# Router logits taken from the rows before the first layer norm, and the first expert's down-projection loads held until the first gather has landed

## The chip, the cores and the metric

One core of a Trainium2 chip runs the whole kernel. The metric is device time in microseconds (us) of one execution; lower is better. The engines are TensorE (PE, with its weight loads listed apart as PEld), VectorE (DVE), ScalarE (ACT), GpSimd (POOL, which here issues transfers and builds gather indices) and SyncE (SP, which here only issues transfers).

## The reference, cut to what matters

Two sequences of 512 rows of 1024 floats go through one encoder layer. The part that the change touches is this:

```python
x = layer_norm(DEEPNORM_ALPHA * x + jnp.dot(mixed, w_out), ln1_g, ln1_b)
x = layer_norm(DEEPNORM_ALPHA * x + grouped_moe(x, ...), ln2_g, ln2_b)

def layer_norm(x, g, b):        # over the 1024 columns of a row
    return (x - mu) * rsqrt(var + 1e-5) * g + b

def grouped_moe(x, w_router, router_bias, w_gate, w_up, w_down):
    scores = sigmoid(dot(x, w_router))          # 16 experts
    ...                                         # best of 4 groups, best 2 experts in it
    for e in range(16):
        h = silu(dot(x, w_gate[e])) * dot(x, w_up[e])
        y = y + combine[:, e:e+1] * dot(h, w_down[e])
```

With y a row ahead of the first norm, w_router the matrix W, and g and b the gain and bias, the router's logits are `rstd * (y @ (g*W) - mean * (g @ W)) + b @ W`: they can be had from the row ahead of the norm, once its mean and its reciprocal root are known.

## The kernel before, in words

All matmuls run on operands that were split into a high and a low float32r part, so each product is three matmuls (high by high, high by low, low by high: lines 1402 to 1404). ACT makes the high part with a cast, DVE the low part with a subtraction.

A sequence is 4 tiles (t = 0..3) of 128 rows. `schedule()` writes one list of events by hand; each engine's program walks this list and issues what the event means on that engine, in that order, so the list is each engine's program order. The two sequences follow one another (s = 0, 1). Within one: 18 weight chunks of projections (`C` events in quarters, with `P` events preparing the next chunk: ACT's cast at L922, DVE's subtraction at L1168), 32 steps p of attention, two heads' blocks each (`S` scores at L1437, maximum on DVE at L1178 or L1192, exponential on ACT at L945 or L950, `T` transposes of the probabilities at L1547 with their copy by ACT at L540, `PV` at L1572), and the output projection (`W` events: 2 halves of 512 columns x 4 weight chunks `pi` x 4 tiles; six matmuls each). Behind the last chunk of a half, `Y` events on DVE add the projection to the residual row in `x_nat` (L1272) and take its statistics (L1275).

The layer norm is a `VAR` event (DVE: mean and variance of 4 tiles, L1301 and L1302, and a chain of small instructions for the reciprocal root, L1127 to L1132) and four `LN` events (DVE, L1309 and L1310, 1024 columns each; POOL then stores the tile to `x1_dram`, L830). In ACT's program the `LN` events of sequence 1 carry the casts of the first expert's first 8 weight units (L931).

The router of a tile is three units: two `r` units (PE transposes four 128-column blocks of the normed row into a PSUM bank, L1466; ACT copies the bank to `x1T`, L1027) and one `R` unit (8 matmuls by `wr`, L1582, which the trace lists as 16; ACT copies 16 logits to `sc`, L1037). These units share two PSUM banks T0 and T1 in rotation with the `T` units, and a unit waits until ACT has emptied its bank. For sequence 0 the router's units stand in steps 2 to 10 of sequence 1; for sequence 1 they stand behind its `LN` events. Then ACT takes the sigmoid of all logits (L1040), and DVE's `routing` (L590 to L675) builds the index lists; its first instruction waits for the sigmoid and for all stores of `x1_dram`.

Behind it comes the expert stage. POOL copies the first indices (L849) and gathers 128 rows of 1024 floats from `x1_dram` into `x_nat` (L846). PE transposes them (L1608), ACT and DVE split them (L1046, L1325), and PE runs the 48 gate and up matmuls (L1402 to L1404) and the 24 down matmuls (L1644) of a tile. An expert's weights are 12 units of 512 KB: 4 of `w_gate`, 4 of `w_up` (units 0 to 7), 4 of `w_down` (units 8 to 11). There is one raw buffer for each unit: SP loads unit w of expert e+1 (L713, L717) when DVE has split unit w of expert e (L1319). SP's issues are in order. For the first expert, units 0 to 7 are loaded during the attention of sequence 1, and unit 8 waits for the index lists:

```python
                if w == KD:
                    sp.wait_ge(routed, 1)
                load_unit(0, w)
```

At the end the experts' outputs are gathered back, combined and normed, and the rows are stored.

Of the kernel before, what the change touches and what calls it, by code (L numbers as in the profile page):

```python
# [89 lines left out]
def schedule():  # L90
# [42 lines left out]
    for s in range(NSEQ):  # L133
# [10 lines left out]
        for p in range(NP + 1):  # L144
# [68 lines left out]
        for pi in range(4):  # L213
# [13 lines left out]
    return ev, tu[0]  # L227


EVENTS, N_TU = schedule()  # L230
# [8 lines left out]
R_UNITS = {(s, t): [e[4] for e in EVENTS if e[0] == "r" and e[1:3] == (s, t)] for s in range(NSEQ) for t in range(NT)}  # L239


def build_kernel(nc, x, mem, w_in, w_mem_kv, sink, rpb, grp_g, w_out, ln1_g, ln1_b, w_router, router_bias,
                 w_gate, w_up, w_down, ln2_g, ln2_b, out):
    with ExitStack() as ctx:
# [77 lines left out]
        mvv = sb("mvv", [P, 12, 2])  # L322
# [4 lines left out]
        sc = sb("sc", [P, TT, NE])  # L327
        idxc = sb("idxc", [P, 1], I32)
# [73 lines left out]
        x1_stored = sem("x1_stored")  # L402
        sig_done = sem("sig_done")
# [164 lines left out]
        def routing(dve, link):  # L568
# [19 lines left out]
            dve.wait_ge(sig_done, 1)  # L588
# [92 lines left out]
        def _(sp):  # L681
# [65 lines left out]
        def _(pool):  # L747
# [50 lines left out]
            for ev in EVENTS:  # L798
# [32 lines left out]
                elif what == "R" and s == 0 and ev[2] == NT - 1:  # L831

                    pool.wait_ge(x1_stored, 16 * NT)
                    for t in range(NT):
                        for u in R_UNITS[(0, t)]:
                            pool.wait_ge(t_ready[u % 2], u // 2 + 1)
                        pool.dma_start(x_nat[:, t, :], x[1][t * P:(t + 1) * P, :]).then_inc(x_again[t], 16)
# [70 lines left out]
        def _(act):  # L908
# [48 lines left out]
            for ev in EVENTS:  # L957
# [64 lines left out]
                elif what == "r":  # L1022
                    t, b, u = ev[2], ev[3], ev[4]
                    act.wait_ge(t_ready[u % 2], u // 2 + 1)
                    if t == 0 and b == 0:
                        act.wait_ge(vb_stored, 16 * 8 * (s + 1))
                    nc.scalar.activation(x1T[t % 2][:, 4 * b:4 * b + 4, :], Tb[u % 2][:, :].rearrange("p (k c) -> p k c", k=4),  # L1027
                                         ACT.Copy).then_inc(t_drained[u % 2], 1)
                elif what == "LN" and s == NSEQ - 1:
# [3 lines left out]
                    hi_units(0, 0, (2 * t, 2 * t + 1))  # L1033
                elif what == "R":
                    t, u = ev[2], ev[3]
                    act.wait_ge(t_ready[u % 2], u // 2 + 1)
                    nc.scalar.copy(sc[:, s * NT + t, :], Tb[u % 2][:, 0:NE]).then_inc(t_drained[u % 2], 1)  # L1037
# [78 lines left out]
        def _(dve):  # L1116
# [87 lines left out]
            for ev in EVENTS:  # L1204
# [94 lines left out]
                elif what == "VAR":  # L1299
                    for t in range(NT):  # L1300
                        link(nc.vector.bn_aggr(mvv[:, t, :], stats[:, t, :, :].rearrange("p a b -> p (a b)")))  # L1301
                    link(nc.vector.tensor_scalar(nv[:, 0:NT], mvv[:, 0:NT, 1], EPS, None, ALU.add))  # L1302
                    rsqrt(rstd[:, s * NT:(s + 1) * NT], NT)
                elif what == "LN":
# [4 lines left out]
                    link(nc.vector.scalar_tensor_tensor(row, row, mvv[:, t, 0:1], ln[:, 0, :], ALU.subtract, ALU.mult))  # L1309
# [87 lines left out]
        def _(pe):  # L1397
# [43 lines left out]
            for ev in EVENTS:  # L1441
                what, s = ev[0], ev[1]
                if what in ("x", "m", "oA", "oM", "oB", "r"):
# [18 lines left out]
                    else:  # L1462
                        pe.wait_ge(x1_ready, s * NT + t + 1)
                        src = [x_nat[:, t, (4 * ev[3] + k) * P:(4 * ev[3] + k + 1) * P] for k in range(4)]
# [110 lines left out]
                elif what == "R":  # L1575
# [4 lines left out]
                    pe.wait_ge(t_drained[u % 2], u // 2)  # L1580
                    for k in range(KD):
# [95 lines left out]
```

## Time and profile before

| | us |
|---|---|
| median of 3 runs | 1092.63 |
| the 3 runs | 1094.33, 1087.12, 1092.63 |
| time of the profiled execution | 1090.34 |
| its span in the profile | 1088.8 |
| busy in the span: PE / DVE / ACT / POOL | 908.7 / 636.7 / 522.3 / 138.3 |

The profile is of one execution. Times in it count from the start of the span; the time of the execution is 1.5 us longer than the span. Matmuls are pipelined: a row gives how long one was in the array, and the step from one start to the next is shorter.

### The profile page before, as it was taken

The page shows a single profiled execution, that of the slowest core. Times are in us where ns is not written, and L with a number is a line of the kernel's source. Part 1 is how long each engine was busy: PE and PEld are TensorE (multiplying, and loading weights), DVE is VectorE, ACT ScalarE, POOL GpSimd, SP SyncE. Part 2 cuts the span into 40 slices and gives each one's busy share as a digit, 9 for nine tenths or more (in the row PEclk, how much of TensorE's full clock was granted, in tenths as well). Part 3 has the DMA queues.
Part 4 walks back from the last instruction along what each step waited for, and adds up shares of the span by engine and source line. Part 5 has one row for each costly group of instructions (what it writes and reads, how often), then busy time and mean ns, then how long its engine had stood idle before and what let it go on. Part 6 is the DMA issues. An engine that isn't in the chain of part 4 may idle for free.

```text
span 1088.8 us, 15827 instructions
## 1 busy us (share of the span) xinstructions
PE 908.7 (83%) x4892; PEld 754.1 (69%) x4893; DVE 636.7 (58%) x1184; ACT 522.3 (48%) x974; POOL 138.3 (13%) x202
## 2 busy tenths in 40 slices
PE   6799999899799999896619999999999999998000
PEld 6677888778688887775617788787878787877000
DVE  5335545466364445566368888875457664461696
ACT  4334554533355555533108787855447464452310
POOL 3200010010000010000010000000000000003775
PEclk9999999899999999898558999999999999999555
DMA  7822132053334123025259999995676966656811
GB/s 233 149 42 71 47 85 90 20 193 99 89 85 155 40 79 97 20 68 191 90 185 337 393 396 401 391 395 175 210 259 219 352 204 228 210 193 223 316 79 77
DMA packets 113404, 195.58 MB, mean 180 GB/s; under 512 B 23137, under 2 KB 52032, under 8 KB 113360
## 3 DMA queue, kind: packets, MB, share of 16 engines
q1 hardware_dynamic: 97296, 139.48, 37.4%
q0 software_dynamic: 12752, 43.47, 12.2%
q10 hardware_dynamic: 3312, 12.06, 2.7%
q8 instruction: 25, 0.41, 0.2%
q14 instruction: 19, 0.16, 0.0%
HBM read 167.71 MB, written 27.65 MB: 179 GB/s over the span
## 4 chain that ended last, share of the span: by engine, by line
PE 55%; DVE 11%; ACT 2%; DMA 2%; issue 2%; POOL 0%; ACTq 0%; DVEq 0%; POOLq 0%
PE O L1644 12%; PE C L1402 10%; PE C L1403 10%; PE C L1404 10%; PE O L1572 3%; PE T L1608 2%; PE T L1582 2%; PE S L1437 2%; DVE mixing L1375 1%; PE T L1547 1%; PE T L1466 1%; DVE mixing L1374 1%; DVE split_aux L1340 1%; DMA x_nat<-x_dram,idxc 1%; ACT split_aux L1059 1%
## 5 line engine op out<-in xcount | busy, mean ns | idle before, releaser
L1319 DVE TENSOR_TENSOR split_main<-mixing,split_main 128x1024 fp32r<-128x1024 f32 x192 | 220.8, 1218 | 50.7 <-ACT split_main L931 50.1
L931 ACT CAST split_main<-mixing 128x1024 fp32r<-128x1024 f32 x192 | 189.4, 1048 | 34.0 <-PE C L1404 18.3
L1402 PE MATMUL C<-split_main,split_aux 128*128 128x512 f32 x368 | 144.3, 392 | 2.6 <-DVE split_aux L1325 2.6
L1644 PE MATMUL O<-split_main,split_aux 128*128 128x512 f32 x552 | 132.3, 395 | 16.2 <-DVE split_aux L1340 16.2
L1404 PE MATMUL C<-split_main,split_aux 128*128 128x512 f32 x368 | 144.1, 392 | 0.0
L1403 PE MATMUL C<-split_main,split_aux 128*128 128x512 f32 x368 | 144.1, 392 | 0.0
L1402 PE MATMUL C<-split_main 128*128 128x512 f32 (+1 forms) x320 | 129.6, 405 | 9.7 <-DVE split_main L1219 6.3
L1644 PEld LDWEIGHTS O<-split_main,split_aux 128*128 128x128 f32 x552 | 101.8, 188 | 42.4 <-DVE split_aux L1340 21.6
L1403 PE MATMUL C<-split_main 128*128 128x512 f32 (+1 forms) x320 | 121.0, 378 | 0.0
L1404 PE MATMUL C<-split_main 128*128 128x512 f32 (+1 forms) x320 | 120.6, 377 | 0.0
L1402 PEld LDWEIGHTS C<-split_main 128*128 128x128 f32 x320 | 62.7, 196 | 28.8 <-issue 10.9
L1402 PEld LDWEIGHTS C<-split_main,split_aux 128*128 128x128 f32 x368 | 69.7, 190 | 17.5 <-issue 3.0
L1404 PEld LDWEIGHTS C<-split_main,split_aux 128*128 128x128 f32 x368 | 69.7, 189 | 14.6
L1403 PEld LDWEIGHTS C<-split_main,split_aux 128*128 128x128 f32 x368 | 69.7, 189 | 14.5
L540 ACT COPY probsT<-T 128x256 f32<-128x256 f32 (+1 forms) x128 | 46.0, 401 | 60.9 <-PE T L1547 59.2
L950 ACT ACTIVATE probs<-probs,negm 128x256 f32<-128x256 f32 (+1 forms) x96 | 51.5, 538 | 49.0 <-DVE negm L1192 49.0
L1404 PEld LDWEIGHTS C<-split_main 128*128 128x128 f32 x320 | 62.2, 194 | 11.3
L1403 PEld LDWEIGHTS C<-split_main 128*128 128x128 f32 x320 | 62.7, 196 | 8.2
L1192 DVE CUSTOM_DVE_ANT_0 probs<-S,mixing,nsink 128x256 f32<-128x256 f32 (+1 forms) x64 | 32.7, 548 | 56.3 <-PE S L1437 56.1
L1168 DVE TENSOR_TENSOR split_main<-mixing,split_main 128x1024 fp32r<-128x1024 f32 x36 | 44.0, 1225 | 36.4 <-ACT split_main L922 36.3
L1335 DVE TENSOR_TENSOR x_nat<-x_nat,C 128x256 f32<-128x256 f32 x46 | 17.3, 417 | 70.7 <-PE C L1404 70.7
L1059 ACT CAST split_aux<-S 128x256 fp32r<-128x256 f32 x46 | 14.9, 375 | 85.1 <-PE S L1633 85.1
(240 smaller groups left out, 1409.0 us busy)
## 6 DMA issues: line engine op xcount, KB each, us to landing
mixing<-in_w_gate SPq DMA_DIRECT2D x64, 512.0 KB, 7.7
mixing<-in_w_up SPq DMA_DIRECT2D x64, 512.0 KB, 5.6
mixing<-in_w_down SPq DMA_DIRECT2D x64, 512.0 KB, 7.3
y_dram<-x_nat ACTq DMA_DIRECT2D x23, 512.0 KB, 6.7
mixing<-in_w_in SPq DMA_DIRECT2D x20, 512.0 KB, 3.8
mixing<-in_w_out SPq DMA_DIRECT2D x16, 512.0 KB, 3.8
y_dram<-x_nat POOLq DMA_DIRECT2D x18, 256.0 KB, 4.3
mixing<-in_w_mem_kv SPq DMA_DIRECT2D x8, 512.0 KB, 3.8
```

What stands on the lines that cost most here:

```text
L540: copy(probsT[:, a % 2, 0:w], Tb[u % 2][:, 0:w]).then_inc(t_drained[u % 2], 1)
L931: nc.scalar.copy(wu[0][:, w, :], raw[:, w, :]).then_inc(unit_hi, 1)
L950: nc.scalar.activation(pr[:, 0:w], pr[:, 0:w], ACT.Exp, scale=-1.0, bias=negm[:, gi % 2, j:j + 1], accum_out=sums[:, gi % 2, j:j + 1]).the ...
L1059: nc.scalar.copy(dst, src).then_inc(hT_hi, 1)
L1168: ins = nc.vector.tensor_tensor(wch[1][:, slot, :, :], wraw[:, slot], wch[0][:, slot, :, :].bitcast(F32), ALU.subtract)
L1192: nc.vector.tensor_tensor_reduce(out=probs[:, a % 2, 0:w], in0=Sb[a % 2][:, 0:w], in1=bias, scale=-1.0, scalar=start, op0=ALU.add, op1=ALU ...
L1319: nc.vector.tensor_tensor(wu[1][:, w, :], raw[:, w, :], wu[0][:, w, :].bitcast(F32), ALU.subtract).then_inc(unit_lo, 1)
L1402: ins = nc.tensor.matmul(out_ap, st[0], mvg[0], start=first, stop=False)
L1403: ins = nc.tensor.matmul(out_ap, st[0], mvg[1], start=False, stop=False)
L1404: ins = nc.tensor.matmul(out_ap, st[1], mvg[0], start=False, stop=last)
L1572: ins = nc.tensor.matmul(Ob[gi % 2][:, j * HD:(j + 1) * HD], probsT[:, a % 2, k * P:(k + 1) * P], v, start=(k == 0), stop=(k == len(vs) - 1))
L1644: ins = nc.tensor.matmul(Ob[half][:, :], st[a_], wu[b_][:, KD + f, half * 512:(half + 1) * 512], start=(f == 0 and a_ + b_ == 0), stop=(f ...
```

## The change

The router's units work on `x_nat` ahead of the norm. In sequence 1's tail they stand between the last `W` events, a tile's `r` units one tile behind its projection and its `R` unit two behind, and `VAR` and `LN` come after all of them. The router's weights are `wr` times the gain (`wrg`); a pseudo sequence `GB`, whose two tiles are the gain and the bias, already broadcast over the partitions, gives the gain's columns and the two constants `g @ W` and `b @ W` (`scon`). It runs in steps 0 to 2 of sequence 1. Sequence 0's own units move to steps 3 to 10, a tile's two `r` units in the same step, and `VAR` from step 1 to 2, its `LN` from 1, 3, 5, 7 to 4, 6, 8, 10. An `SC` event corrects the logits on DVE in four instructions of 128x64: for sequence 0 at step 12, for sequence 1 between `LN` of tile 0 and `LN` of tile 1; in ACT's program the sigmoid of all logits stands there too. A sigmoid of one column (`warm`) is put ahead of ACT's first router copy of sequence 1. SP's wait ahead of unit 8 of the first expert is for the first gather instead of the index lists. The order of POOL's issues changes in one place only (the reload of `x_nat` goes from behind the last `R` of sequence 0 to behind its last `LN`).

```diff
@@ schedule(), in the steps p of a sequence
             if s > 0:
-                if p == 1:
+                if p < 2:
+                    router(GB, p, 0)
+                    router(GB, p, 1)
+                if p in (1, 2):
+                    router(GB, p - 1, 2)
+                if p == 2:
+                    ev.append(("GW", s))
                     ev.append(("VAR", s - 1))
                 for t in range(NT):
-                    if p == 2 * t + 1:
+                    if p == 2 * t + 3:
+                        router(s - 1, t, 0)
+                        router(s - 1, t, 1)
+                    if p == 2 * t + 4:
+                        router(s - 1, t, 2)
                         ev.append(("LN", s - 1, t))
-                    if 0 <= p - (2 * t + 2) < 3:
-                        router(s - 1, t, p - (2 * t + 2))
+                if p == 12:
+                    ev.append(("SC", s - 1))
@@ schedule(), the end of a sequence and of the list
-        for pi in range(4):
+        for pi in range(3 if s + 1 == NSEQ else 4):
             wo(s, 1, pi, WO_ORDER[1], True)
...
-    ev.append(("VAR", NSEQ - 1))
+    s = NSEQ - 1
+    for t in range(NT + 2):
+        if t < NT:
+            wo(s, 1, 3, (t,), t == NT - 1)
+        if t > 0 and t - 1 < NT:
+            router(s, t - 1, 0)
+            router(s, t - 1, 1)
+        if t > 1:
+            router(s, t - 2, 2)
+    ev.append(("VAR", s))
     for t in range(NT):
-        ev.append(("LN", NSEQ - 1, t))
-    for t in range(NT + 1):
-        if t < NT:
-            for b in range(2):
-                router(NSEQ - 1, t, b)
-        if t > 0:
-            router(NSEQ - 1, t - 1, 2)
+        ev.append(("LN", s, t))
+        if t == 0:
+            ev.append(("SC", s))
@@ routing (DVE)
-            dve.wait_ge(sig_done, 1)
+            dve.wait_ge(sig_done, 2)
@@ loads of the first expert (SP)
                 if w == KD:
-                    sp.wait_ge(routed, 1)
+                    sp.wait_ge(xg_loaded, 16)
@@ ACT
+                    if s == NSEQ - 1 and t == 0 and b == 0:
+                        act.wait_ge(vb_stored, 16 * 8 * NSEQ)
+                        nc.scalar.activation(warm[:, :], seed[:, 0:1], ACT.Sigmoid).then_inc(sig_done, 1)
                     nc.scalar.activation(x1T[t % 2][:, 4 * b:4 * b + 4, :], ..., ACT.Copy).then_inc(t_drained[u % 2], 1)
...
+                elif what == "SC" and s == NSEQ - 1:
+                    act.wait_ge(logits_ready, NSEQ)
+                    nc.scalar.activation(sc[:, :, :], sc[:, :, :], ACT.Sigmoid).then_inc(sig_done, 1)
...
-            for b in range(2):
-                act.wait_ge(t_drained[b], (N_TU - 1 - b) // 2 + 1)
-            nc.scalar.activation(sc[:, :, :], sc[:, :, :], ACT.Sigmoid).then_inc(sig_done, 1)
@@ DVE
+                elif what == "GW":
+                    t_waits(dve, R_UNITS[(GB, 0)][1])
+                    nc.vector.tensor_tensor(wrg[:, :, :], wr[:, :, :], x1T[0][:, :, 0:1].to_broadcast([P, KD, NE]), ALU.mult)\
+                        .then_inc(gains_ready, 1)
+                elif what == "SC":
+                    t_waits(dve, T_OF_R[(s, NT - 1)])
+                    raw_, mean = sc[:, s * NT:(s + 1) * NT, :], mvv[:, 12:12 + NT, 0]
...
+                    link(nc.vector.tensor_tensor(sct, over_t[0], mean, ALU.mult))
+                    link(nc.vector.tensor_tensor(sct, raw_, sct, ALU.subtract))
+                    link(nc.vector.tensor_tensor(sct, sct, rs, ALU.mult))
+                    nc.vector.tensor_tensor(raw_, sct, over_t[1], ALU.add).then_inc(logits_ready, 1)
                 elif what == "LN":
                     t = ev[2]
+                    for u in R_UNITS[(s, t)]:
+                        dve.wait_ge(t_ready[u % 2], u // 2 + 1)
@@ PE
-                        pe.wait_ge(x1_ready, s * NT + t + 1)
-                        src = [x_nat[:, t, ...] for k in range(4)]
+                        if s == GB:
+                            pe.wait_ge(ln_loaded, 32)
+                        else:
+                            pe.wait_ge(wo_drained, wo_done(s, 1, t))
+                        rows = (ln if s == GB else x_nat)[:, t, :]
+                        src = [rows[:, ...] for k in range(4)]
...
-                        ins = nc.tensor.matmul(Tb[u % 2][:, 0:NE], x1T[t % 2][:, k, :], wr[:, k, :],
+                        ins = nc.tensor.matmul(Tb[u % 2][:, 0:NE], x1T[t % 2][:, k, :], (wr if s == GB else wrg)[:, k, :],
```

## Rows read from the trace of the kernel before

**Rows 1.** The page, the span in 40 slices of 27.2 us: granted clock and DMA share.
```profile
PEclk9999999899999999898558999999999999999555
DMA  7822132053334123025259999995676966656811
```

**Rows 2.** Timeline, tail of sequence 1 (start, us; in brackets the idle time before).
```profile
503.18 0.39 PE L1402 MATMUL S<-split_main 128*128 128x512 f32 x1
...
505.34 0.69 DVE L1272 SCALAR_TENSOR_TENSOR x_nat<-x_nat,S 128x512 f32<-128x512 f32 x1
...
506.79 0.94 DVE L1301 BATCH_NORM_AGGREGATE mvv<-stats 128x2 f32<-128x12 f32 x4
...
510.14 1.28 DVE L1309 SCALAR_TENSOR_TENSOR x_nat<-x_nat,mvv,ln 128x1024 f32<-128x1024 f32 x1
...
517.27 3.57 PE L1582 MATMUL T<-wr,vstg 128*128 128x16 f32 x16
...
519.01 1.28 DVE L1310 SCALAR_TENSOR_TENSOR x_nat<-x_nat,rstd,ln 128x1024 f32<-128x1024 f32 x1
...
535.10 1.28 ACT L1040 ACT_TABLE_LOAD   x1
```

**Rows 3.** Timeline, from the routing's start to the first expert's matmuls.
```profile
537.04 0.48 DVE L590 MEMSET x_nat<- 128x512 f32 x1 [16.20 <-ACT sc L1040]
...
556.47 0.06 DVE L675 MEMSET seed<- 128x1 f32 x1
556.56 2.01 SPq L717 DMA_DIRECT2D mixing<-in_w_down  x4
...
558.00 1.72 POOL L846 DMA_INDIRECT x_nat<-x_dram,idxc  x1 [0.29 <-POOL idxc L849]
...
568.03 1.94 PE L1608 MATMUL T<-ident,x_nat 128*128 128x128 f32 x8 [12.07 <-DMA x_nat<-x_dram,idxc]
...
572.53 0.79 PE L1402 MATMUL C<-split_main,split_aux 128*128 128x512 f32 x1 [2.57 <-DVE split_aux L1325]
```

**Rows 4.** Chain that ended last, two of its pieces (start, us, what).
```profile
558.00 9.89 DMA x_nat<-x_dram,idxc
...
588.13 5.78 PE O L1644 x24
```

**Rows 5.** Windows: busy us (and count) of PE, PEld, DVE, ACT, POOL, then clock, DMA, GB/s.
```profile
296.00:298.00 2.00, 0.27 (x2) 0.15 (x2) 1.48 (x3) 0.77 (x3) 0.00 (x0) 1.00 0.01 2
...
508.00:510.00 2.00, 0.00 (x0) 0.00 (x0) 1.66 (x11) 2.00 (x3) 0.00 (x0) 0.87 0.00 0
510.00:512.00 2.00, 0.00 (x0) 0.00 (x0) 1.93 (x3) 2.00 (x3) 0.00 (x0) 0.50 0.00 0
...
574.00:576.00 2.00, 2.00 (x6) 1.62 (x5) 2.00 (x3) 1.98 (x2) 0.00 (x0) 0.50 0.95 355
```

**Rows 6.** Timeline, sequence 0's router units in the steps of sequence 1.
```profile
308.65 0.60 ACT L1027 ACTIVATE vstg<-T 128x512 f32<-128x512 f32 x1
...
311.77 0.60 PE L1466 MATMUL T<-ident,x_nat 128*128 128x128 f32 x4
...
317.00 1.85 PE L1582 MATMUL T<-wr,vstg 128*128 128x16 f32 x16
```

**Rows 7.** Waits of PE from 293 to 350 us (in total, times, longest).
```profile
PE T L1547 <- ACT probs L945: 1.7, 1, 1.7
PE T L1547 <- ACT vstg L1027: 0.9, 1, 0.9
```

**Rows 8.** Windows, 300 to 350 us (columns as in rows 5).
```profile
300.00:350.00 50.00, 49.14 (x340) 41.95 (x340) 27.86 (x56) 26.80 (x74) 4.24 (x8) 1.00 0.33 107
```

**Rows 9.** DMA issues from 500 to 545 us (count, KB each, median us to landing).
```profile
x_dram<-x_nat POOLq DMA_DIRECT2D x4, 512.0 KB, 3.0
```

**Rows 10.** DMA issues from 555 to 600 us.
```profile
x_nat<-x_dram,idxc POOLq DMA_INDIRECT x3, 6.6
```

**Rows 11.** DMA from 600 to 640 us, all queues.
```profile
DMA packets 6442, 16.01 MB, mean 400 GB/s; under 512 B 488, under 2 KB 488, under 8 KB 6441
```

**Rows 12.** Timeline of ACT, the second expert's weight casts.
```profile
589.07 5.93 ACT L931 CAST split_main<-mixing 128x1024 fp32r<-128x1024 f32 x6 [0.20 <-issue]
```

More of the change, by code:

```diff
@@ L238 @@
 LAST_M = [max(e[4] for e in EVENTS if e[0] == "m" and e[1] == s) for s in range(NSEQ)]
-R_UNITS = {(s, t): [e[4] for e in EVENTS if e[0] == "r" and e[1:3] == (s, t)] for s in range(NSEQ) for t in range(NT)}
+R_UNITS = {(s, t): [e[4] for e in EVENTS if e[0] == "r" and e[1:3] == (s, t)] for s in range(NSEQ + 1) for t in range(NT)}
 def build_kernel(nc, x, mem, w_in, w_mem_kv, sink, rpb, grp_g, w_out, ln1_g, ln1_b, w_router, router_bias,
@@ L327, in build_kernel @@
         sc = sb("sc", [P, TT, NE])
+        wrg = sb("wrg", [P, KD, NE])
+        scon = sb("scon", [P, 2, NE])
+        sct = sb("sct", [P, NT, NE])
+        warm = sb("warm", [P, 1])
         idxc = sb("idxc", [P, 1], I32)
@@ L830, in _ @@
                     pool.dma_start(x1_dram[(s * NT + t) * P:(s * NT + t + 1) * P, :], x_nat[:, t, :]).then_inc(x1_stored, 16)
[L831 to L837, printed above, removed]
+                    if s == 0 and t == NT - 1:
+                        pool.wait_ge(x1_stored, 16 * NT)
+                        for t in range(NT):
+                            pool.dma_start(x_nat[:, t, :], x[1][t * P:(t + 1) * P, :]).then_inc(x_again[t], 16)
             pool.dma_start(ln[:, 0, :], ln2_g.partition_broadcast(P)).then_inc(ln2_loaded, 16)
@@ L1300, in _ @@
                     for t in range(NT):
-                        link(nc.vector.bn_aggr(mvv[:, t, :], stats[:, t, :, :].rearrange("p a b -> p (a b)")))
-                    link(nc.vector.tensor_scalar(nv[:, 0:NT], mvv[:, 0:NT, 1], EPS, None, ALU.add))
+                        link(nc.vector.bn_aggr(mvv[:, 12 + t, :], stats[:, t, :, :].rearrange("p a b -> p (a b)")))
+                    link(nc.vector.tensor_scalar(nv[:, 0:NT], mvv[:, 12:12 + NT, 1], EPS, None, ALU.add))
                     rsqrt(rstd[:, s * NT:(s + 1) * NT], NT)
+                elif what == "GW":
[5 more added lines that the diff above has]
+                    raw_, mean = sc[:, s * NT:(s + 1) * NT, :], mvv[:, 12:12 + NT, 0]
+                    rs = rstd[:, s * NT:(s + 1) * NT]
+                    over_t = [scon[:, i, :].unsqueeze(1).to_broadcast([P, NT, NE]) for i in range(2)]
+                    link(nc.vector.tensor_tensor(sct[:, :, :], over_t[0], mean.unsqueeze(2).to_broadcast([P, NT, NE]), ALU.mult))
+                    link(nc.vector.tensor_tensor(sct[:, :, :], raw_, sct[:, :, :], ALU.subtract))
+                    link(nc.vector.tensor_tensor(sct[:, :, :], sct[:, :, :], rs.unsqueeze(2).to_broadcast([P, NT, NE]), ALU.mult))
+                    nc.vector.tensor_tensor(raw_, sct[:, :, :], over_t[1], ALU.add).then_inc(logits_ready, 1)
                 elif what == "LN":
                     t = ev[2]
+                    for u in R_UNITS[(s, t)]:
+                        dve.wait_ge(t_ready[u % 2], u // 2 + 1)
                     if s == 0 and t == 0:
@@ L1462, in _ @@
                     else:
-                        pe.wait_ge(x1_ready, s * NT + t + 1)
-                        src = [x_nat[:, t, (4 * ev[3] + k) * P:(4 * ev[3] + k + 1) * P] for k in range(4)]
+                        if s == GB:
[3 more added lines that the diff above has]
+                        rows = (ln if s == GB else x_nat)[:, t, :]
+                        src = [rows[:, (4 * ev[3] + k) * P:(4 * ev[3] + k + 1) * P] for k in range(4)]
                     for k, part in enumerate(src):
```

16 lines of the change are left out of this document (11 added, 5 removed).

## The prediction

> **What bounds the kernel now.** I read the page's slices first. PE's clock stands at its high level nearly everywhere, and the one deep hole ahead of the end is the 20th and 21st, 517 to 571 us [rows 1]. So I read the timeline there. The last six matmuls of the output projection start at 503.18 and PE's dense work is over 1.4 us later, at 504.6: 24 such matmuls take 5.78 us, 0.24 each [rows 4]. It begins again with the first expert at 572.53 [rows 3]. These 68 us are one serial path, and what the change does to the time is decided there. Its first part, from the last `Y` on DVE (505.34) to the routing's first instruction (537.04), takes 31.7 us: `Y` 1.45, `VAR` from 506.79 to 510.14, four `LN` from 510.14 to 520.29, then the router's units at PE's half clock, with 3.57 us for 16 entries of `R`, and a table load of 1.28 ahead of the sigmoid [rows 2, 3]. DVE waits 16.2 us for that sigmoid [rows 3]. The second part is the routing on DVE, 537.04 to 556.5, which stays as it is. The third is the first gather, 9.89 us from issue to landing, with the transposes and splits behind it [rows 3, 4]. PE waits 12.07 us for it. The gather is issued 1.4 us behind four loads of `w_down`, on other queues [rows 3].
>
> The other place that the change touches is the start of sequence 1's attention. There PE is the bound: busy 49.14 of 50 us from 300 to 350, with only 2.6 us of waits from 293 to 350 [rows 7, 8]. Work added to PE there costs its full length; DVE (27.86 of 50) and ACT (26.80) have room.
>
> **Part 1, the tail of sequence 1.** At the high clock, `r` is four transposes of 0.60 together and `R` 1.85, both less some 0.15 that runs on under the next instruction (0.39 in the array against a step of 0.24): 0.45 and 1.70. ACT's copy of a bank is 0.60 [rows 2, 4, 6]. Ahead of the last tile's matmuls PE now does `r` twice for tiles 0 and 1 and `R` of tile 0: 4 x 0.45 + 1.70 = 3.5. Two banks serve them all, so the second pair waits for ACT, whose first copy is behind the new table load (1.28 and a short sigmoid); most of that load passes under tile 2's matmuls, and I put 1.1 for the waits. So the last matmul ends at 504.6 + 4.6 = 509.2 and the last `Y` starts at 509.35, 4.0 later than before. From there: `Y` 1.45, `VAR` 3.35, `LN` of tile 0 2.55, to 516.7. PE meanwhile does `r` twice for tiles 2 and 3, `R` three times and some bank waits, 7.7 us, and its last logits are out at 517.3; DVE waits 0.7 for them. Four small `SC` instructions: 1.0 (estimate; the trace of before has none of 128x64). Three `LN`: 7.6. Then POOL's store of the last tile, 0.35 until it is issued and 3.0 to its landing [rows 9], which was hidden under the router before and is now what ends last. That is 509.35 + 1.45 + 3.35 + 2.55 + 0.7 + 1.0 + 7.6 + 3.35 = 529.4 against 537.04: **7.6 us less**. The sigmoid is not late: the two casts ahead of it on ACT and itself take some 2.3 us, while DVE is in its three `LN`. POOL's queue has nothing ahead of the store. Bounds: 5 (waits on the banks doubled, `SC` twice as long) to 9.5 (no bank waits, store landing in 2).
>
> The clock decides whether these units cost 0.45 and 1.70 or twice that. In the tail of before PE stood still from 504.9, and its clock fell only between 508 and 510 (mean 0.87), to the low level from 510 [rows 5]. A stop of 1.7 us at 296 left it at 1.00 [rows 5]. In the changed order no stop is that long until the last `R`, so I count with the high level.
>
> **Part 2, the first gather alone.** With SP's wait, the four `w_down` loads and the second expert's loads behind them on SP start after the landing. The store of the same 512 KB lands in 3.0 with nothing beside it [rows 9]; three gathers of this kernel under load have a median of 6.6 [rows 10]. Alone it lies between 3.0 and 6.6; I take 3.5, near the lone store, with 0.5 for the longer issue (1.72 [rows 3]): **6.4 us less** (3.3 to 6.9).
>
> A rule of the Trainium skill speaks against so much: in DMA: Bandwidth & Descriptors (section Queues, rings and completion order) each DMA engine goes round the queues that have work, packet by packet. By it the gather would get about half of the engines beside SP's stream, and holding the loads would save only the other half; that is the first rival below.
>
> What the hold costs: the loads start at the landing G instead of some 11 us ahead of it, and PE starts 4.6 us behind G (572.53 - 567.89 [rows 3, 4]). A unit of 0.524 MB takes 1.31 us at the 400 GB/s of rows 11. The last unit of the second expert is the seventeenth transfer (16 units, one gather): G + 17 x 1.31 + 1.7 for the landing (3.0 - 1.31 [rows 9]) = G + 24. ACT cast the last of these units some 21.5 us behind PE's start [rows 3, 12], G + 26. So it is 2 us in time; at the 355 GB/s seen from 574 to 576 [rows 5] it is 17 x 1.48 + 1.7 = G + 26.9, 0.9 late. I put 0.5 lost (0 to 4).
>
> **Part 3, gain and bias through the router's units.** Four `r` and two `R` more on PE: 4 x 0.45 + 2 x 1.70 = 5.2. Two `r` fall into PE's wait of 1.7 at step 0 [rows 7], 0.9 back; but the first probabilities then wait for ACT's two copies, about 1.0, and the first `R` for its bank, 0.5. The stop of 0.9 behind an `r` copy [rows 7] goes, since no `r` stands in step 2 any more. Together **4.8 us more**. Bounds: 2.6 (all of rows 7 filled) to 8 (0.6 more in each of the four steps with two `r`, where a copy is behind a weight cast on ACT). `GW` (0.3), `SC` (1.0) and the later `VAR` and `LN` lie in DVE's free half [rows 8]. PE stays the bound from there to the sequence's end, so the shift passes through.
>
> **The sum.** 7.6 + 6.4 - 4.8 - 0.5 = 8.7 us less than the profiled execution's 1090.34 (span 1088.8 and 1.5 around it): 1081.6. This execution is 2.3 under the median of the runs, 1092.63; from the median it is 1083.9. I say 1082.5.
>
> **Rivals.** (a) The gather was slow by itself, not by its neighbours: for it speaks its POOL time of 1.72 and that gathers between loads have 6.6, not 9.9 [rows 3, 10]; against it the lone store's 3.0. At half of 400 GB/s for 0.524 MB the neighbours cost 1.3: 1090.34 - 7.6 - 1.3 + 4.8 + 0.5 = 1086.7.
> (b) The clock falls in the tail, as it did before: the units between and behind the projection then take twice as long, 3.5 + 7.7 more, and the last projection tiles 2.8. The last logits come near 528.5 instead of 517.3, and DVE's `SC`, three `LN` and the store end at 540.5, 3.5 later than before: 1090.34 + 3.5 - 6.4 + 4.8 + 0.5 = 1092.7, no gain. Against it: rows 5, as above.
> (c) The other side: the weights become the bound of the expert stage. An expert with one tile moves 12 units, a gather and a store, 14 x 0.524 = 7.34 MB, while PE needs 72 x 0.24 = 17.3 and about 1.3 for transposes and waits, 18.6. So below 395 GB/s the transfers are slower than PE. Before, they ran ahead by what was loaded during the gather; that lead is what the change spends. At 355 to 365 GB/s an expert takes 20.4, 1.8 more, and the six full slices of DMA, the 22nd to the 27th [rows 1], hold about 9 of them: 16 us, 1090.34 - 8.7 + 16 = 1097.6. Against it: 400 GB/s held over 40 us [rows 11].
> (d) The shift of part 3 is at its upper end and the tail's waits on two banks at theirs: 5 + 6.4 - 8 - 0.5, 1087.4.
>
> **Chances.** Forecast 0.63, (a) 0.12, (b) 0.07, (c) 0.06, (d) 0.12. The forecast's own range is 1076 to 1088; with (a), (b) and (d) the range is 1075 to 1092. A difference of 1%, 10.9 us, is about what a measurement of this kernel can tell from no change. The forecast lies just inside it, and about half of its spread beyond: faster 0.34; slower 0.05, of (c); same 0.61.
>
> **What would show it.** Right: matmuls of the router between those of the last projection tiles, at clock 1.00 until 516; the routing's first instruction near 529, released by a store; the gather at 3 to 4 us; `w_down` issued behind its landing; no wait of PE for DVE's weight splits in the first three experts; the first scores behind step 3 some 5 us later than before. Wrong: the sigmoid still releasing the routing, a gather above 6, PE waiting on L1319 in the expert stage, or a clock of 0.50 before 516.

## The result and the profile after

| | before | after |
|---|---|---|
| median | 1090.70 us (17 runs) | 1096.09 us (17 runs) |
| lowest to highest | 1087.12 to 1094.74 | 1092.87 to 1100.62 |
| profiled execution, its span | 1090.34, 1088.8 | 1095.57, 1093.8 |

The changed kernel takes 1.0047 of the time before, with a 95% interval of 1.0033 to 1.0061: 5.4 us slower by the medians, where 8 to 10 less had been forecast, and outside the range. The two profiled executions differ by as much, 5.0 of span. Cut at the same events, the two traces say where:

| stretch | before | after | difference | forecast |
|---|---|---|---|---|
| start to the first scores of sequence 1 | 293.9 | 297.8 | +3.9 | 0 |
| first scores of step 0 to those of step 12 | 67.0 | 73.7 | +6.7 | +4.8 |
| step 12 to the first `Y` of the tail | 139.8 | 140.5 | +0.7 | 0 |
| first `Y` to the routing's first instruction | 36.4 | 32.0 | -4.4 | -7.6 |
| the routing | 19.4 | 19.4 | 0 | 0 |
| routing's end to the transposes of the gathered rows | 11.6 | 6.5 | -5.1 | -6.4 |
| from there to the first expert's first matmul | 4.5 | 4.5 | 0 | 0 |
| that matmul to PE's last of the experts | 431.7 | 435.5 | +3.8 | +0.5 |
| the end | 84.6 | 84.0 | -0.7 | 0 |

The first line is in code that the change doesn't touch. There the clock fell once more in this execution (from 94 to 100 us it was at 0.50); other executions of the same code have that fall (experiments 4 and 6) or not (1 and 3). It is a reminder that a term of 2 us can't be read from one execution's end time, only at its own place.

**The tail.** Timeline of the kernel after, PE and DVE mixed (answers to rows 2; columns as there):

```profile
516.77 1.93 PE L1627 MATMUL T<-wrg,vstg 128*128 128x16 f32 x16 [0.34 <-ACT vbw L1050]
...
520.27 0.69 DVE L1296 SCALAR_TENSOR_TENSOR x_nat<-x_nat,S 128x512 f32<-128x512 f32 x1 [3.21 <-PE S L1443]
...
524.58 3.57 PE L1627 MATMUL T<-wrg,vstg 128*128 128x16 f32 x16 [0.34 <-ACT vbw L1050]
527.99 3.57 PE L1627 MATMUL T<-wrg,vbw 128*128 128x16 f32 x16
...
531.88 0.23 DVE L1337 TENSOR_TENSOR sct<-scon,mvv 128x64 f32<-128x64 f32 x1 [4.19 <-ACT sc L1064]
...
543.95 0.48 DVE L612 MEMSET x_nat<- 128x512 f32 x1 [2.99 <-issue]
```

The first two `R` units take 1.93 us, the last two 3.57: the clock has halved ahead of them. DVE, which had finished the first `LN`, stands 4.19 us in front of `SC` for the last logits; the three `LN` and the store come behind that. The windows of PE in the same stretch (start:end, length, busy and count, granted clock, DMA share, GB/s) show when it fell:

```profile
520.00:522.00 2.00, 1.66 (x15) 1.00 0.00 0
522.00:524.00 2.00, 2.00 (x20) 1.00 0.00 0
524.00:526.00 2.00, 1.66 (x10) 0.54 0.00 0
526.00:528.00 2.00, 2.00 (x12) 0.50 0.00 0
```

and finer ones show that it fell in front of the third `R` (524.58):

```profile
524.10:524.20 0.10, 0.10 (x2) 0.78 0.00 0
524.20:524.30 0.10, 0.04 (x1) 0.50 0.00 0
```

PE had no stop over 0.34 us between 516 and 531. Still the clock went from 2.4 to 1.2 GHz at 524. For what releases the routing the profile of after names nothing (`issue`). The last store is issued at 540.72 and lands 3.0 later by the median, at 543.7, so I take it to be the store, as in experiments 3 and 11, where the profile names it.

**The gather and the first expert.** The chain that ended last, of after (start, us, what; answers to rows 4):

```profile
564.92 4.82 DMA x_nat<-x_dram,idxc
572.15 8.86 DMA mixing<-in_w_gate
581.11 1.28 ACT L951
```

and the timeline of after behind it (answers to rows 3):

```profile
569.88 1.94 PE L1653 MATMUL T<-ident,x_nat 128*128 128x128 f32 x8 [7.00 <-DMA x_nat<-x_dram,idxc]
...
577.16 1.05 ACT L951 CAST split_main<-mixing 128x1024 fp32r<-128x1024 f32 x1 [1.60 <-DMA mixing<-in_w_down]
...
587.61 0.60 ACT L1077 ACTIVATE x_nat<-C 128x512 f32<-128x512 f32 x1
...
590.79 0.77 PE L1678 MATMUL S<-ident,x_nat 128*128 128x128 f32 x4 [2.27 <-DVE x_nat L1374]
592.15 7.31 PE L1689 MATMUL O<-split_main,split_aux 128*128 128x512 f32 x24 [0.59 <-DVE split_aux L1379]
```

The gather takes half of the 9.89 it took before. But right behind it in the chain stands a weight load, which was not there before, of the second expert's first gate unit: ACT's casts of the first expert's four down units and then of this unit wait for their transfers, they stand ahead of the first silu (587.61) in ACT's program, and PE waits 2.27 us for what follows from the silu. After that stop the clock falls again (it is at 0.50 from 592.4 to 595.8), and the 24 down matmuls take 7.31 instead of 5.78 [rows 4].

**The steps of sequence 1.** Timeline of PE, of after:

```profile
299.89 1.03 PE L1509 MATMUL T<-ident,ln 128*128 128x128 f32 x8
302.81 0.90 PE L1590 MATMUL T<-ident,probs 128*128 128x128 f32 x4 [1.88 <-ACT vstg L1050]
...
308.44 1.93 PE L1627 MATMUL T<-wr,vstg 128*128 128x16 f32 x16 [0.34 <-ACT vbw L1050]
...
315.12 1.85 PE L1627 MATMUL T<-wr,vbw 128*128 128x16 f32 x16
```

From one step's first scores to the next, steps 0 to 2 take 5.81, 8.03 and 6.60 where they took 4.78, 4.79 and 6.27.

### The profile page after: what moved, and what is told of

Read it like the earlier page. It is cut to its first block, busy times and chain, and to the rows that moved or that the text cites. A ratio compares the mean times of both kernels' runs of the same rounds, so it can differ in the third digit from the quotient of the medians.

```text
span 1093.8 us, 15953 instructions
## 1 busy us (share of the span) xinstructions
PE 914.6 (84%) x4940; PEld 758.4 (69%) x4941; DVE 638.9 (58%) x1193; ACT 524.3 (48%) x981; POOL 138.6 (13%) x202
## 4 chain that ended last, share of the span: by engine, by line
PE 55%; DVE 10%; ACT 3%; issue 2%; DMA 2%; POOL 0%; SPq 0%; DVEq 0%; ACTq 0%; POOLq 0%
PE O L1689 12%; PE C L1441 10%; PE C L1442 9%; PE C L1443 9%; PE O L1615 3%; PE T L1627 2%; PE T L1653 2%; PE S L1476 2%; PE T L1590 1%; DVE mixing L1414 1%; DVE mixing L1413 1%; PE T L1509 1%; DVE split_aux L1379 1%; DMA mixing<-in_w_gate 1%; ACT split_aux L1083 1%
## 5 line engine op out<-in xcount | busy, mean ns | idle before, releaser
L1441 PE MATMUL C<-split_main 128*128 128x512 f32 (+1 forms) x320 | 131.0, 409 | 9.7 <-DVE split_main L1243 6.3
L1442 PE MATMUL C<-split_main 128*128 128x512 f32 (+1 forms) x320 | 122.6, 383 | 0.0
L1443 PE MATMUL C<-split_main 128*128 128x512 f32 (+1 forms) x320 | 121.9, 381 | 0.0
L1441 PEld LDWEIGHTS C<-split_main 128*128 128x128 f32 x320 | 63.4, 198 | 29.0 <-issue 11.1
L1442 PEld LDWEIGHTS C<-split_main,split_aux 128*128 128x128 f32 x368 | 69.7, 189 | 14.5
L1443 PEld LDWEIGHTS C<-split_main 128*128 128x128 f32 x320 | 63.4, 198 | 11.7
L1442 PEld LDWEIGHTS C<-split_main 128*128 128x128 f32 x320 | 63.5, 198 | 8.4
L1192 DVE TENSOR_TENSOR split_main<-mixing,split_main 128x1024 fp32r<-128x1024 f32 x36 | 44.0, 1225 | 36.4 <-ACT split_main L942 36.3
```

The costliest lines, as they stand in the source:

```text
L1192: ins = nc.vector.tensor_tensor(wch[1][:, slot, :, :], wraw[:, slot], wch[0][:, slot, :, :].bitcast(F32), ALU.subtract)
L1441: ins = nc.tensor.matmul(out_ap, st[0], mvg[0], start=first, stop=False)
L1442: ins = nc.tensor.matmul(out_ap, st[0], mvg[1], start=False, stop=False)
L1443: ins = nc.tensor.matmul(out_ap, st[1], mvg[0], start=False, stop=last)
```

## The experiments

The diffs are against the kernel after, where nothing else is said. The medians of before beside them are 1090.5 to 1090.8.

**1. The change without the hold on the loads.**

```diff
-                    sp.wait_ge(xg_loaded, 16)
+                    sp.wait_ge(routed, 1)
```

> The changed kernel with SP's old wait, so that the first expert's down-projection loads start with the index lists. My theory: the hold shortened the first gather by 5.0 us (9.89 to 4.84) and gave 3.8 back in the first expert (PE waits 2.3 for DVE, then 1.5 at the low clock), so undoing it makes the kernel 1 us slower, 0 to 2.5, with a gather of 9 to 10 us and no wait of PE for the gated row in the first expert. Rival, the prediction's: the hold is worth 6, and the kernel is 5 to 6 us slower without it. Second rival: the later start of the weights costs more over the experts behind it than the gather gains, and the kernel is 1 us or more faster without the hold.

1094.9 us median of 12, 1.0031 of before (1.0011 to 1.0051): 1.2 less than after, not more, though the two intervals overlap, so this doesn't show a gain either. The gather is slow again (11.0 us from the routing's end to the transposes) and the experts take 430.7 instead of 435.5. So the hold's two sides roughly cancel.

**2. The hold alone, on the kernel before.**

```diff
-                    sp.wait_ge(routed, 1)
+                    sp.wait_ge(xg_loaded, 16)
```

> The kernel before with SP's new wait alone. My theory: a gather near 4.8 us instead of 9.9, a wait of PE of some 2 us in the first expert, and in all 1 us faster than the kernel before, 0 to 2.5. Rival, the prediction's: 5 to 6 us faster. Second rival: slower than the kernel before.

1090.7 median of 12, 0.9999 (0.9982 to 1.0017). The gather takes 4.92 instead of 9.89, and the experts 436.4 instead of 431.7. Timeline of this kernel, ACT and PE in its first expert:

```profile
570.73 1.04 ACT L931 CAST split_main<-mixing 128x1024 fp32r<-128x1024 f32 x1 [0.58 <-DMA mixing<-in_w_down]
573.17 1.06 ACT L931 CAST split_main<-mixing 128x1024 fp32r<-128x1024 f32 x1 [1.39 <-DMA mixing<-in_w_down]
...
577.26 1.28 ACT L931 ACT_TABLE_LOAD   x1 [1.77 <-DMA mixing<-in_w_gate]
...
586.95 0.85 PE L1633 MATMUL S<-ident,x_nat 128*128 128x128 f32 x4 [2.85 <-DVE x_nat L1335]
588.30 8.53 PE L1644 MATMUL O<-split_main,split_aux 128*128 128x512 f32 x24 [0.51 <-DVE split_aux L1340]
```

The same waits as in after, without any other part of the change. All of the loss is in the first expert: from its first matmul to the second expert's it takes 26.2 us (570.51 to 596.67), where before took 21.2 (572.53 to 593.75). Part of it is the clock: behind the stop it fell here (587.5 to 594.3) and for a shorter time in after (24.9 us for the same stretch), and in experiment 5, which has the hold too, not at all (23.5).

**3. The correction behind all four layer norms.** The `SC` event goes from behind the first `LN` to behind the last, and ACT's sigmoid goes ahead of its first casts.

```diff
     for t in range(NT):
         ev.append(("LN", s, t))
-        if t == 0:
-            ev.append(("SC", s))
+    ev.append(("SC", s))
```

> The changed kernel with sequence 1's SC behind all four LN, and ACT's casts of the first expert's units behind the sigmoid. My theory: in the changed kernel DVE stood 4.2 us between LN of tile 0 and SC, because the last logits came late (two R at the low clock), and SC itself took 1.0; behind the LN both pass under the last store of x1. So 4.5 us faster than the changed kernel, 3.5 to 5.5, the routing released by the store. Rival: the wait for the logits is not what sets the routing's start, or ACT's casts become late for the first expert: within 1 us of the changed kernel.

1090.84 median of 12, 0.9995 (0.9978 to 1.0011): 5.3 less than after. From the first `Y` to the routing it takes 26.8 us instead of 32.0. Timeline of DVE:

```profile
529.94 0.22 DVE L1334 TENSOR_TENSOR sct<-scon,mvv 128x64 f32<-128x64 f32 x1
...
533.55 0.48 DVE L611 MEMSET x_nat<- 128x512 f32 x1 [2.08 <-DMA x_dram<-x_nat]
```

No wait stands ahead of `SC` any more: the logits come while DVE norms. The store's landing is last.

**4. The gain's and bias's units on the kernel before**, in its steps 0 to 2, with their results unused.

```diff
+                if p < 2:
+                    router(GB, p, 0)
+                    router(GB, p, 1)
+                if p in (1, 2):
+                    router(GB, p - 1, 2)
```

> The kernel before with the four r and two R units of gain and bias added in steps 0 to 2 of sequence 1, their results unused. My theory: in the changed kernel the scores of step 12 moved 6.7 us against those of step 0, so this costs 5.5 to 7, by PE's own 5.2 and by waits for ACT's copies. Rival, the prediction's: 4.8, 4 to 5. Second rival: the 6.7 come from the double r units of sequence 0's tiles, and the addition alone costs 3 to 4.

1096.81 median of 10, 1.005 (1.0032 to 1.0067), 6.0 more than before. Steps 0 to 2 take 5.81, 8.00 and 8.51, the later ones what they took before: 1.03 + 3.21 + 2.24 more, 6.5. Of step 2's part some 1.5 is the clock (an estimate: with such a fall this step takes 8.12 in experiment 1, and 6.60 in after without it). Windows of PE:

```profile
308.00:310.00 2.00, 1.66 (x16) 1.00 0.00 0
310.00:312.00 2.00, 2.00 (x20) 1.00 0.00 0
312.00:314.00 2.00, 2.00 (x13) 0.68 0.51 209
314.00:316.00 2.00, 2.00 (x6) 0.50 0.13 53
```

**5. Experiment 3, with the last four projection tiles ahead of all router units.**

```diff
+    wo(s, 1, 3, WO_ORDER[1], True)
     for t in range(NT + 2):
-        if t < NT:
-            wo(s, 1, 3, (t,), t == NT - 1)
```

> The changed kernel with SC behind all LN, as in the run before, and with the last four projection tiles ahead of all router units. My theory: the router units between the tiles put the last Y off (8.3 us from first to last Y, 4.7 in the kernel before); with the tiles first, Y, VAR and the four LN start 3.6 earlier, the router's units pass beside them on PE, at whichever clock, and the store of the last tile releases the routing some 23 us behind the first Y, against 26.8 with SC last alone. So 3 to 4.5 us faster than SC last alone, 5 below the kernel before. Rival: with no wide matmuls between them the router's units all run at the low clock and the last logits come behind the store: within 1.5 us of SC last alone.

1087.02 median of 11, 0.9962 (0.9945 to 0.998), and 22.95 us from the first `Y` to the routing (510.64 to 533.59). That is the time that was expected, but not by the store: the clock fell here too, at 522, and the last logits release the routing. Timeline of DVE:

```profile
531.88 0.22 DVE L1333 TENSOR_TENSOR sct<-scon,mvv 128x64 f32<-128x64 f32 x1 [1.93 <-ACT sc L1060]
```

Router work between the projection's tiles had cost 3.8 us (26.8 to 22.95): it delayed the last `Y`, and with it `VAR` and all `LN`, for logits that are not due before the last of them.

**6. Wide matmuls in the tail.** Six matmuls of 128x512, into a bank that nothing reads, ahead of each of the last two `R` units of after.

```diff
+                    if s == NSEQ - 1 and t >= 2:
+                        for k in range(6):
+                            nc.tensor.matmul(Cb[0][:, :], xT[0][:, k, 0:P], xT[0][:, k, :], start=(k == 0), stop=(k == 5))
```

> The changed kernel with six more matmuls of 128x512, whose result nobody reads, ahead of each of the last two R units of the tail. My theory: in the changed kernel the clock fell between 517 and 524 while PE was listed busy at 83% or more, with transposes and 16-column matmuls alone, so it is what they are and not a stop that drops it. With the wide ones between them the clock stays at 1.00 until the last R, each R takes 1.9 instead of 3.57, and the last logits come within 1 us of where they were, 19.6 behind the first Y, although 2.7 us of work were added. Rival: the clock falls there anyway, by the short stops for ACT's copies, and the last logits come 2.7 us later.

1096.44 median of 4, 1.0072 (1.0044 to 1.01). The time says nothing; the run was made for its trace. Timeline and windows of PE:

```profile
524.69 1.63 PE L1628 MATMUL C<-split_main 128*128 128x512 f32 x6 [0.34 <-ACT vbw L1050]
526.16 1.85 PE L1630 MATMUL T<-wrg,vstg 128*128 128x16 f32 x16
527.86 1.65 PE L1628 MATMUL C<-split_main 128*128 128x512 f32 x6
529.34 1.85 PE L1630 MATMUL T<-wrg,vbw 128*128 128x16 f32 x16
```

```profile
524.00:526.00 2.00, 1.66 (x10) 1.00 0.00 0
526.00:528.00 2.00, 2.00 (x19) 1.00 0.00 0
```

The busy time of both windows is the same as in after, and so is the stop of 0.34; the clock is 1.00 instead of 0.54 and 0.50. But this comparison doesn't show that the wide matmuls did it. Up to 524.58 the two programs issue the same instructions (here some 0.1 us later), and the clock of after had fallen by then, at 524.2: the two executions differ before the edit can act. Nor were there narrow matmuls "alone" from 517 to 524, as I had expected: six wide ones of the projection run from 518.54 to 520.18. What the trace does show is that the clock stays at 1.00 through the wide matmuls and the last two `R`. Each `R` gains 1.7 and pays 1.5 for the six matmuls ahead of it, so `SC` starts at 531.51 instead of 531.88.

**7. The constants without the units.** Gain and bias come in once more as columns (two small transfers at the start), two DVE multiplications make `g * W` and `b * W`, and 16 matmuls by a matrix of ones in sequence 0 make the two constants. The `GB` units go.

```diff
+                    for i, w_ in enumerate((wrg, wrb)):
+                        for k in range(KD):
+                            ins = nc.tensor.matmul(Ob[0][:, i * NE:(i + 1) * NE], ones_f, w_[:, k, :],
+                                                   start=(k == 0), stop=(k == KD - 1))
```

> The changed kernel with gain and bias as columns by two small transfers and the two constants by 16 matmuls of ones by the weights, in PE's stop of 3.2 us ahead of the seventh chunk of the first sequence's projections, instead of the four r and two R units in steps 0 to 2 of sequence 1. My theory: those units cost 5.0 and now and then a fall of the clock; without them the steps 0 to 12 of sequence 1 take 68.5 us instead of 73.6, the 1.6 above the 67.0 of the kernel before being the double r units, and the kernel is 5 to 6.5 us faster than the changed one. Rival: the additional units filled waits and the loss came from the double r units: 1 to 3 us faster.

1094.64 median of 11, 1.0024 (1.0007 to 1.0041): only 1.5 less than after. In the profiled execution steps 0 to 2 take 4.77, 6.34 and 4.77, so the units' cost is gone there, but step 0 to step 12 takes 73.7 all the same: the clock fell at 301, at 318 and at 362. Step 1, 6.34 instead of 4.79, holds the first of these falls. Step 3 takes 6.73 (after: 4.86), with a stop of PE of 1.72 in it: DVE's `VAR`, which the change has moved here, stands ahead of this step's maxima, so the exponentials come late and, behind them in ACT's program, the copies of the two `r` units. The first two falls came behind stops of 1.73 and 1.72. The third came without any stop; windows of PE:

```profile
354.00:356.00 2.00, 2.00 (x18) 1.00 0.00 0
356.00:358.00 2.00, 2.00 (x16) 1.00 0.17 41
358.00:360.00 2.00, 2.00 (x15) 1.00 0.74 221
360.00:362.00 2.00, 2.00 (x20) 1.00 0.00 0
362.00:364.00 2.00, 2.00 (x14) 0.55 0.65 262
```

PE is busy in all of the 8 us up to 362, from 359 on with an `R` unit, matmuls of 64 columns and transposes. The theory's size isn't borne out by the time, and why the clock falls there in some kernels and executions and not in others stays open.

**8. What the first seven suggest, together:** the columns, sequence 0's router units one step apart as before, the projection's tiles first, the correction last, no hold.

> All that the runs point to: constants from columns, one router unit in each step of sequence 1 as in the kernel before, the last projection tiles ahead of the router's units, SC and sigmoid behind all LN, the down-projection loads started with the index lists. My theory: steps 0 to 12 take 67 us as before, the routing starts 23 us behind the first Y instead of 36.4, the gather and the experts are as before: 12 to 14 us faster than the kernel before. Rival: without the router's wait the stores or ACT's casts of the first expert's units set the next limit, and less than 9 us is left.

1084.31 median of 6, 0.9943 (0.9926 to 0.996): 6.5 less than before, where 12 to 14 were expected. From the first `Y` to the routing it took 24.5 and not 23: with no projection tiles between the units the clock fell at 513, three of the four `R` units took 3.57, and DVE waited 3.46 us for the last logits behind its fourth `LN`. Steps 0 to 12 took 69.7, with one fall of the clock in step 4 (8.54 instead of 6.97).

**9 and 10. Half of the hold:** the first expert's down weights are loaded at the end of the index lists, as before, and only the second expert's loads wait for the gather. On experiment 8, and alone on the kernel before:

```diff
                 load_unit(0, w)
+            sp.wait_ge(xg_loaded, 16)
             with sp.Fori(1, NE) as e:
```

> The kernel of the earlier run with columns, single router units, the projection's tiles first and the correction last (1084.31 median), with one wait more on SP: the four loads of the first expert's down weights go at the end of the index lists, as before, and only the second expert's loads wait for the first gather. Theory W (the hold loses its gain because the first expert's own down weights come late: ACT casts them, in its program, ahead of the first silu): the gather has four transfers beside it instead of some twelve and takes 6 to 8 us from issue (alone 4.84, beside all 9.89), the four casts of the down weights do not wait, and from the first matmul of the first expert to PE's last of the stage it takes 431 to 433 us; 2 to 4 less than 1084.3, about 1081.5. Rival Q (what the hold loses is the lead over the second expert and later ones): the stage takes 434 or more, and the time stays within 1 of 1084.3. Rival N (the gather is slow beside any four loads): it takes 9 to 10 us and nothing changes but the second expert's later loads.

> The kernel before with that wait alone: down weights of the first expert at once, the second expert's loads behind the first gather. W: gather 6 to 8 us instead of 9.89, the expert stage 431 to 433 us long; 1087.5 to 1089 against 1090.8. Q: gather as in W, stage 434 or more, 1090 to 1091.5. N: gather 9 to 10, 1090 to 1092.

On experiment 8: 1081.66 median of 4, 0.99 (0.9866 to 0.9933), with a gather of 8.39 and an expert stage of 432.2. On before: 1088.45 median of 10, 0.9975 (0.9957 to 0.9992), 2.0 under the median beside it. The chain's gather row and then the timeline of experiment 10:

```profile
558.38 8.32 DMA x_nat<-x_dram,idxc
```

```profile
569.78 3.89 ACT L932 CAST split_main<-mixing 128x1024 fp32r<-128x1024 f32 x4
...
581.04 0.60 ACT L1054 ACTIVATE x_nat<-C 128x512 f32<-128x512 f32 x1
...
586.10 5.78 PE L1645 MATMUL O<-split_main,split_aux 128*128 128x512 f32 x24 [0.70 <-DVE split_aux L1341]
```

The four casts of the down weights run without a wait, the first silu is 9.7 us behind the first matmul (571.35) instead of 13.2 in after (574.39 to 587.61), and the stage takes 430.8. That is what theory W expects, and rival Q falls. It doesn't single out the down units, though: with them loaded early the second expert's gate units have four transfers fewer ahead of them, and their casts don't wait for a transfer either. W's size for the gather was off: with four loads beside it, it takes 8.3, more than the 6 to 8 expected.

**11. Two wide matmuls ahead of each `R` of the tail**, on experiment 9, in PE's waits for ACT's copies.

```diff
+                    if s == NSEQ - 1:
+                        for k in range(2):
+                            nc.tensor.matmul(Cb[0][:, :], xT[0][:, k, 0:P], xT[0][:, k, :], start=(k == 0), stop=(k == 1))
```

> The half hold with the columns kernel, and two wide matmuls (128x512, into a bank that nothing reads) ahead of each of the four R units of the tail, in PE's wait for ACT's copy: 8 x 0.23 = 1.8 us of PE work added, of which the four waits of 0.34 hide 1.2. Six such matmuls ahead of two units kept the clock at 1.00 through the tail. If two are enough too, the R units take 1.8 to 1.95 us each instead of 3.57, the last logits are out before DVE's fourth layer norm ends, the routing starts some 23 behind the first projection add instead of 24.5 (now by the store's landing), and the time is 1 to 2 less than the half hold alone. If the clock falls all the same (R at 3.57), the time is 0.5 to 1.5 more.

1080.95 median of 4, 0.99 (0.9865 to 0.9936). Timeline of PE and DVE:

```profile
520.08 0.70 PE L1633 MATMUL C<-split_main 128*128 128x512 f32 x2
520.66 1.93 PE L1638 MATMUL T<-wrg,vstg 128*128 128x16 f32 x16
522.44 0.71 PE L1633 MATMUL C<-split_main 128*128 128x512 f32 x2
522.99 1.85 PE L1638 MATMUL T<-wrg,vbw 128*128 128x16 f32 x16
...
530.42 0.48 DVE L611 MEMSET x_nat<- 128x512 f32 x1 [2.05 <-DMA x_dram<-x_nat]
```

All four `R` units stay at the high clock, and the routing starts 22.8 us behind the first `Y`, now by the store. By the medians it is 0.7 less than experiment 9, where 1 to 2 were expected, and their intervals don't separate the two; the trace shows the place. In experiment 9 the clock fell at 515.8, 5.4 us behind the last `Y` (510.38); here the first wide matmuls run 1.8 behind it (513.75, `Y` at 511.94), so in this pair the edit can act before the fall. It is one execution of each. This is the fastest kernel of the study, 1% below the kernel before.

## Why the prediction was wrong

**Part 1, the tail: -4.4 for -7.6.** The order of events came as described, and most terms held: the last `Y` moved by 3.6 within the tail (4.0 forecast), `SC` took 0.9 (1.0), and the store's landing is what released the routing (3.5 for 3.35). The step that failed is "In the changed order no stop is that long until the last `R`, so I count with the high level". I took stops as the one thing that makes the clock fall, because the one fall that I had read began behind a stop [rows 5]. In after it fell with no stop over 0.34 us, under transposes and 16-column matmuls, so "DVE waits 0.7" for the last logits became 4.19. That is rival (b), which I had priced with the clock falling from the start of the tail (3.5 more); it fell only for the last two `R` units. (The price of (b) had two slips: its 2.8 for the last projection tiles is named and not added, and its 1092.7 lies outside the range that was to hold it.)

That a stop isn't needed is shown by experiment 7, whose clock fell at 362 with PE busy all the time before it. What makes it fall is not settled. In the seven profiled executions with the router's units between projection and norm and no wide matmuls among them (after, experiments 1, 3, 5, 7, 8 and 9) it fell before the last `R` was over; in the two with wide matmuls (6 and 11) it did not. That fits the wide matmuls having kept it, but it doesn't prove it: in experiment 6 the difference to after was there ahead of the edit, and in experiment 11 the wide matmuls also fill PE's waits for ACT. The Trainium skill, TensorE: Matmul & The Clock Gate (section A second HAM failure mode: psum-queue depth-cycling), describes a clock that swings because PE idles briefly between groups of matmuls; the fall at 362 in experiment 7 came without such idle times, so they can't be all of it here.

The other half of this step is where `SC` stood. Behind the first `LN` its wait for PE stops three `LN` and a store that need nothing of it; behind the last it costs next to nothing (experiment 3, 5.3 less). I had computed that wait, 0.7, and did not ask what a longer one would cost there.

**Part 2, the gather: -5.1 for -6.4, and 3.8 given back for 0.5.** Alone the gather takes 4.82, not 3.5; a lone store of the same bytes was the wrong row to take it from. Rival (a) fell: neighbours cost 5 us, not 1.3. The rule on the DMA queues from which 1.3 came (the Trainium skill, DMA: Bandwidth & Descriptors, section Queues, rings and completion order, quoted ahead) does not give these sizes with my reading of it, an equal share for the gather: it took 4.82 alone, 8.32 beside four loads and 9.89 beside all of them.

The step that failed is "The last unit of the second expert is the seventeenth transfer ... So it is 2 us in time". I looked at the last transfer of the batch. The first ones are due first: by the same formula (G is the landing of the gather) the fifth, the second expert's first gate unit, lands at G + 5 x 1.31 + 1.7 = G + 8.25, and ACT had wanted it 2.3 behind PE's start, at G + 6.9. In after it came at G + 11.3 (569.74 to 581.01). The casts' waits put the five landings near G + 3.4, 4.8, 7.4, 9.1 and 11.3, in order but not 1.31 apart: between G and 581.01 the engines moved 3.54 MB at 314 GB/s, not 400, and only 2.62 of them were these five units, the rest the second gather and later loads. So what is issued beside and behind a transfer puts it off: the median from issue to landing between 555 and 600 us is 11 to 12 us on SP's loads in after, and 5.5 to 7.8 in experiment 1. What is behind these casts is the first silu. Rival (c) named the right resource and the wrong place: the later experts lost nothing (from the second to the third 18.64 us, before and after). Experiments 2, 9 and 10 show that it is the first transfers of the batch.

**Part 3, gain and bias: +6.7 for +4.8.** Steps 0 to 2 rose by 4.6 in after, and by 6.5 in experiment 4 with its fall of the clock, so the six units were sized rightly (the terms add to 4.9, not 4.8). What failed is the move of sequence 0's work: I kept the pairing of its `r` units as a bound ("0.6 more in each of the four steps with two `r`") and took nothing for it, and nothing for "the later `VAR` and `LN`", which were to lie in DVE's free half. Steps 3 to 10 rose by 2.0 in sum, from 46.0 to 48.0: the four with two `r` units by 3.3, while the four with an `R` fell by 1.2. No run tests the pairing alone. Experiment 8 has the later `VAR` and `LN` without it, and without the some 1.6 of its fall of the clock its steps 0 to 12 still take 1.1 more than before, so not all of the 2.0 need be the pairing's; in step 3 of experiment 7 the stop behind `VAR` is seen itself. Rival (d) had this part at 8, nearer to what came.

**The sum.** With the measured terms it is 1090.34 - 4.4 - 5.1 + 3.8 + 6.7 + 0.7, that is 1092.0, and 3.2 more for the untouched ends (+3.9 and -0.7): 1095.2, the profiled 1095.6 within rounding. By medians it closes less well. Experiment 4's 6.0, the 2.0 of the pairs, the tail's -4.4 and nothing for the hold give 3.6 of the measured 5.4; 1.8 are not accounted for, and experiment 7 saved less than its units cost, with the stop behind `VAR` and the falls of its clock. Falls of the clock that differ from execution to execution would do that, but this wasn't shown.

## What to carry to other kernels

A wait belongs behind the work that doesn't need it: the same correction cost 5 us three layer norms too early, and next to nothing behind them. When loads are held back, check the first transfers of the batch against the first instruction that needs one of them, in the program order of the engine that consumes them, and hold only those that are due last. And count PE's time for small matmuls at both clocks, even where PE is never idle.

## What the hardware did unexpectedly

- PE lost its high clock while it was listed busy 1.66 to 2.00 of every 2 us, with transposes and matmuls of 16 columns among its work (after at 524, experiment 4 at 312), and once with no stop in the 8 us before (experiment 7 at 362). In the one profiled execution with two wide matmuls of 0.23 us each ahead of every 16-matmul unit of the tail (experiment 11) it stayed at 1.00 there.
- Executions of the same code differ in where the clock falls. Of sequence 0, which was untouched, the step from the ninth scores to the tenth took 5.2 us in the profile of before and 7.6 in that of after.
- A gather of 512 KB in 128 rows needs 4.82 us alone; its time on POOL is 1.72 of that.
